# Moving most of the adaLN conditioning of a two-block transformer kernel into chunks beside later matrix products, with five smaller edits

## The chip, the cores and the metric

The kernel runs on 1 core of a Trainium2 chip. The metric is the device time of one execution in microseconds (us). A core has TensorE (PE: matrix products into the accumulator memory PSUM), VectorE (DVE), ScalarE (ACT), GpSimd (POOL), each with an instruction queue that is worked through in order, and the queue of SyncE (SP), which here only issues DMA transfers. The engines wait for each other with semaphores. TensorE's clock has two levels, 1.2 and 2.4 GHz; the profile gives the granted clock as a share of the upper one.

## The reference

Two transformer blocks follow each other on x (1 x 512 x 1024). The change touches the first block and a part of the second. The first, cut to what matters:

```python
def first_block(x, c, w_ada, b_ada, ...):
    mod = (silu(c) @ w_ada + b_ada)                    # 1024 -> 6 * 1024
    shift_m, scale_m, gate_m, shift_f, scale_f, gate_f = split(mod, 6)
    h = rmsnorm(x, norm_mix_w) * (1.0 + scale_m) + shift_m
    x = x + gate_m * hybrid_mixer(h, ...)
    h = rmsnorm(x, norm_mlp_w) * (1.0 + scale_f) + shift_f
    return rmsnorm(x + gate_f * (square(relu(h @ w_up)) @ w_down), norm_final_w)

def hybrid_mixer(h, ...):
    z, xbc, dt_raw, u_pool, gate_logits = split(h @ w_in, ...)   # 2048, 3072, 32, 1024, 2048 columns
    xbc = silu(causal_depthwise_conv(xbc, conv_w, conv_b))       # 4 taps
    dt = softplus(dt_raw + dt_bias)
    y = chunked_scan(xbc, dt, a_log) ; y = rmsnorm_by_group((y + d_skip * xs) * silu(z))
    y_ssd = y @ w_branch_ssd                                     # 2048 -> 1024
    pooled = means over windows of 2, 4, 8, 16 rows, minus u     # causal, 256 columns each
    y_pool = ((pooled @ pool_w by group) * pool_scale) @ w_branch_pool
    g_ssd, g_pool = split(sigmoid(gate_logits), 2)
    return (g_ssd * y_ssd + g_pool * y_pool) @ w_out
```

Only shift_m and scale_m are needed at the start; the other four parts of `mod` are first used behind the mixer. The second block is a sparse attention with a convolutional feed-forward, then a differential attention with 8 heads (its keys, values and queries are the product called qkv here) and another feed-forward.

## The kernel before

Activations lie with their features on the 128 partitions and the rows along the free axis. A matrix product is a `Linear` in the table `L`; it is made in groups of 128 output columns, in the order dt, xbc (24 groups), z (16), u (8), gates (16), bs (8), pw (8), bp (8), out, up0, down0, up1, down1, and then the second block. fp32 accuracy comes from three products of split operands: high times high, low times high, high times low. So a group over 1024 inputs is 8 x 3 = 24 matmuls of 512 rows. Each 128-column weight block is a unit: SP loads it into `w_raw` (two buffers), ACT copies its high part into `w_hi` (L428), DVE subtracts to get `w_lo` (L434). All three run two units ahead of TensorE. Counting semaphores keep them in step: `w_split` (a unit is split, its raw buffer free), `units_done` (TensorE has finished a unit), `evacuated` (a PSUM accumulator is free again). `evac_loop` is ACT's side of a product, `post_loop` DVE's, `products` TensorE's; POOL does elementwise work beside them.

The conditioning is `times_c`: the 6144 columns of `w_ada` come in 12 blocks of 512 columns, issued by POOL (L982). For each, DVE forms the sum over 8 row blocks of w times silu(c) in 8 linked steps, one `tensor_scalar` (L615) and seven `scalar_tensor_tensor` (L617); each linked step waits for the one before. TensorE's `modulation` (L1709) then adds over the partitions with four one-column matmuls against ones. Four blocks are made at the start, since h needs them; the other eight are spread over the 24 xbc groups, a third of a block per group. After xbc TensorE does their matmuls and waits for `mod_ready`, then for the last convolution (`conv_out`), and goes on to z. There DVE, POOL and ACT do the scan step by step beside the groups of z; a step needs the decay rows, which SP loads once the last convolution is written.

In gates, ACT's evacuation is a sigmoid (L1280), and POOL does the causal pooling (L1028 to L1036) from the start of the stage. In pw each group has only two row blocks (6 matmuls), but all 8 blocks of its weight buffer are split. ACT scales the accumulator into `et` (L1298), copies the high part (L1301), and DVE subtracts (L2390). qkv's groups all use accumulator banks 0 and 1 (L2033), so each waits for the evacuation of the one before (L1526, L1527). In the differential attention `turn_head` (L2151) transposes a finished head ahead of the next logits, and ACT's `head_out` copies it.

Of the kernel before, what the change touches and what calls it, by code (L numbers as in the profile page):

```python
# [15 lines left out]
P = 128  # L16
# [136 lines left out]
def two_block_program(nc, I, out):  # L153
    ctx = ExitStack()
    with ctx:
# [36 lines left out]
        def pcol(name, i=0):  # L192
# [17 lines left out]
                for i, a in enumerate((A_Z, A_Z + 16384, A_S + 8320, F + 24576))]  # L210
        ADA_FIRST = (2, 3, 0, 1)
        ada_acc = [at(f"ada_acc{i}", [P, 512], F32, A_MISC + (3 + i) * TILE if i < 4 else
                      A_S + 8320 + (i - 4) * 2048 if i < 9 else
                      A_MISC + (6, 3, 4)[i - 9] * TILE) for i in range(12)]
# [297 lines left out]
        def products(pe, l, ready, first=2, between=None, mid=None):  # L512
# [4 lines left out]
            for g in range(first):  # L517
# [91 lines left out]
        def times_c(dve, link, n, k0=0, k1=KD):  # L609

            u, slot, fill = (ADA_FIRST[n], n, 1) if n < 4 else (n, n % 2, n // 2)
            w, acc = wada[slot], ada_acc[u]
            if k0 == 0:
                dve.wait_ge(sem(f"ada_in{slot}"), 16 * fill)
                link(dve.tensor_scalar(acc[:], w[:, 0, :], small[:, 8:9], None, ALU.mult))  # L615
            for k in range(max(k0, 1), k1):
                ins = dve.scalar_tensor_tensor(acc[:], w[:, k, :], small[:, 8 + k:9 + k], acc[:], ALU.mult, ALU.add)  # L617
                if k < KD - 1:
                    link(ins)
                else:  # L620
                    ins.then_inc(sem("ada_acc"), 1)


# [236 lines left out]
        def _(sp):  # L860
# [65 lines left out]

            for name, l in L.items():
                if name == "z":
# [10 lines left out]
                    continue  # L939
                if name in ("ia", "oa1"):  # L940
# [27 lines left out]
        def _(pool):  # L968
# [7 lines left out]

            for n in range(12):
                u, slot = (ADA_FIRST[n], n) if n < 4 else (n, n % 2)
                if n >= 4:

                    pool.wait_ge(sem("ada_acc"), max(4, n - 1))
                pool.dma_start(wada[slot][:], I["w_ada"][0].rearrange("(k p) n -> p k n", p=P)[:, :, u * 512:u * 512 + 512]  # L982
                               ).then_inc(sem(f"ada_in{slot}"), 16)
# [143 lines left out]
        def _(act):  # L1127
            for t in range(NT):
                act.dma_start(xin[:, t, :], I["x"][0, t * P:(t + 1) * P, :]).then_inc(sem(f"x_in{t}"), 16)
            act.dma_start(metain[:], I["meta_tokens_2"]).then_inc(sem("meta_in"), 16)  # L1130
            act.sem_inc(sem("evacuated"), 2)
# [65 lines left out]
            def dt_steps(g):  # L1197
# [4 lines left out]
                elif g == 4:  # L1202
# [3 lines left out]
                elif g == 6:  # L1206
# [6 lines left out]
                elif g == 7:  # L1213
# [3 lines left out]
                      first=8, between=dt_steps, stop=8)  # L1217
            evac_loop(act, L["xbc"], conv_in, conv_silu, start=8)
# [74 lines left out]
            for g in range(KD):  # L1293
                l = L["pw"]
                act.wait_ge(sem("units_done"), l.U0 + g + 1)
                if g >= 2:
                    act.wait_ge(sem("pw_ready"), g - 1)
# [9 lines left out]
            act.wait_ge(sem("pw_ready"), KD)  # L1307
            evac_loop(act, L["bp"], branch_evac("bp"), mixed_hi)
            act.activation(HH[:, :, META - 2:META], modc[:, 24:32].unsqueeze(2).to_broadcast([P, KD, 2]), ACT.Copy)
# [204 lines left out]
            def project_out(g):  # L1514
# [3 lines left out]
                src = PS[:, 0:2, 0:TH]  # L1518
# [90 lines left out]
            for j in range(4):  # L1609
# [24 lines left out]
                for b in range(4):  # L1634
                    if j == 2 and b:
                        head_out(b - 1)
# [1237 lines left out]
```

## Time and profile before

| | |
|---|---|
| median of 3 runs | 2546.71 us (2544.07 to 2549.95) |
| the profiled execution | 2534.87 us, its span 2533.0 us |
| mean granted clock of TensorE | 0.974 |
| busy: PE, PEld, DVE, ACT, POOL | 94%, 84%, 55%, 42%, 16% |
| from HBM | 234.53 MB, 95 GB/s over the span |

The span is the time from the first to the last recorded instruction. PE is TensorE's matmuls, PEld its weight loads, which overlap them. A busy share is an average over stages with different limits; what an edit is worth is read from the stage that it touches.

### The profile page before, as it was taken

The page shows a single profiled execution, that of the slowest core. Times are in us where ns is not written, and L with a number is a line of the kernel's source. Part 1 is how long each engine was busy: PE and PEld are TensorE (multiplying, and loading weights), DVE is VectorE, ACT ScalarE, POOL GpSimd, SP SyncE. Part 2 cuts the span into 40 slices and gives each one's busy share as a digit, 9 for nine tenths or more (in the row PEclk, how much of TensorE's full clock was granted, in tenths as well). Part 3 has the DMA queues.
Part 4 walks back from the last instruction along what each step waited for, and adds up shares of the span by engine and source line. Part 5 has one row for each costly group of instructions (what it writes and reads, how often), then busy time and mean ns, then how long its engine had stood idle before and what let it go on. Part 6 is the DMA issues. An engine that isn't in the chain of part 4 may idle for free.

```text
span 2533.0 us, 41300 instructions
## 1 busy us (share of the span) xinstructions
PE 2392.3 (94%) x15423; PEld 2136.3 (84%) x15423; DVE 1386.4 (55%) x2101; ACT 1062.3 (42%) x1908; POOL 394.1 (16%) x350
## 2 busy tenths in 40 slices
PE   5899988999899999998989999999999989999998
PEld 4678867887689889886868999999878779999987
DVE  5886675423455335457854666643343445766621
ACT  5545863433544234323544433322455545333322
POOL 0000433711320010000121211100100001211100
PEclk8898998999999999999999999999999989999999
DMA  8464332332333353342201323333422112323332
GB/s 279 137 213 116 101 83 59 91 100 75 100 93 91 97 130 98 92 119 52 64 21 48 99 85 89 91 89 89 125 60 62 50 47 80 87 87 91 89 93 92
DMA packets 409384, 238.35 MB, mean 94 GB/s; under 512 B 11338, under 2 KB 400301, under 8 KB 409285
## 3 DMA queue, kind: packets, MB, share of 16 engines
q1 hardware_dynamic: 400453, 202.24, 28.7%
q0 software_dynamic: 8224, 32.61, 3.8%
q10 hardware_dynamic: 608, 2.16, 0.2%
q8 instruction: 64, 1.05, 0.2%
q14 instruction: 35, 0.29, 0.0%
HBM read 234.53 MB, written 5.00 MB: 95 GB/s over the span
## 4 chain that ended last, share of the span: by engine, by line
PE 81%; DVE 7%; ACT 4%; DMA 3%; issue 3%; POOL 0%; SPq 0%; DVEq 0%; POOLq 0%; ACTq 0%
PE PS L507 60%; PE PS L2033 5%; PE PS L1820 3%; DMA w_raw<-in_w_in_dram 1%; DVE ada_acc L617 1%; PE PS L1775 1%; PE PS L2164 1%; PE PS L2069 1%; PE PS L1835 1%; PE PS L2111 1%; ACT w_hi L428 1%; PE PS L1899 1%; DVE w_lo L434 1%; DVE conv_acc L2275 1%; DMA w_ada<-in_w_ada_dram 1%
## 5 line engine op out<-in xcount | busy, mean ns | idle before, releaser
L434 DVE TENSOR_TENSOR w_lo<-w_raw,w_hi 128x1024 fp32r<-128x1024 f32 (+1 forms) x376 | 474.4, 1262 | 637.7 <-ACT w_hi L428 636.5
L507 PE MATMUL PS<-op_hi,w_hi 128*128 128x264 f32 (+4 forms) x2456 | 608.2, 311 | 22.4 <-DVE w_lo L434 11.4
L507 PE MATMUL PS<-op_lo,w_hi 128*128 128x264 f32 (+4 forms) x2456 | 605.3, 310 | 0.0
L507 PE MATMUL PS<-op_hi,w_lo 128*128 128x264 f32 (+4 forms) x2456 | 603.0, 309 | 0.0
L428 ACT ACTIVATE w_hi<-w_raw 128x1024 fp32r<-128x1024 f32 (+1 forms) x376 | 382.8, 1018 | 313.5 <-PE PS L507 261.4
L507 PEld LDWEIGHTS PS<-op_hi,w_hi 128*128 128x128 f32 (+1 forms) x2456 | 399.6, 189 | 56.2 <-DVE w_lo L434 11.3
L507 PEld LDWEIGHTS PS<-op_hi,w_lo 128*128 128x128 f32 (+1 forms) x2456 | 398.9, 189 | 24.6 <-issue 0.8
L507 PEld LDWEIGHTS PS<-op_lo,w_hi 128*128 128x128 f32 (+1 forms) x2456 | 398.7, 189 | 23.4 <-issue 1.4
L507 PE MATMUL PS<-ff_hi,w_lo 128*128 128x512 f32 (+1 forms) x784 | 240.3, 343 | 0.0
L507 PE MATMUL PS<-ff_hi,w_hi 128*128 128x512 f32 (+1 forms) x784 | 239.9, 342 | 0.0
L507 PE MATMUL PS<-ff_lo,w_hi 128*128 128x512 f32 (+1 forms) x784 | 239.9, 342 | 0.0
L1488 ACT ACTIVATE ff_u<-PS 128x528 f32<-128x528 f32 x88 | 53.9, 613 | 334.4 <-PE PS L507 314.2
L603 POOL TENSOR_TENSOR ff_u<-ff_u,rstd 128x528 f32<-128x528 f32 x88 | 100.4, 1142 | 417.3 <-ACT ff_u L1488 389.9
L507 PEld LDWEIGHTS PS<-ff_lo,w_hi 128*128 128x128 f32 x784 | 135.6, 188 | 17.7
L507 PEld LDWEIGHTS PS<-ff_hi,w_lo 128*128 128x128 f32 x784 | 135.4, 188 | 17.7
L507 PEld LDWEIGHTS PS<-ff_hi,w_hi 128*128 128x128 f32 x784 | 135.6, 188 | 17.2
L673 POOL TENSOR_TENSOR sumsq<-sumsq,evac 128x528 f32<-128x528 f32 (+1 forms) x28 | 39.2, 1399 | 535.8 <-ACT evac L646 535.8
L2646 DVE SCALAR_TENSOR_TENSOR ff_c<-ff_u,param_cols,ff_c 128x528 f32<-128x528 f32 x88 | 70.4, 800 | 12.6 <-DVE ff_c L2645 6.7
L2645 DVE SCALAR_TENSOR_TENSOR ff_c<-ff_u,param_cols,ff_c 128x528 f32<-128x528 f32 x88 | 67.7, 769 | 12.7 <-DVE ff_c L2643 6.7
L2643 DVE TENSOR_SCALAR ff_c<-ff_u,param_cols 128x528 f32<-128x528 f32 x88 | 51.1, 580 | 25.7 <-DVE ff_c L2654 14.6
L617 DVE SCALAR_TENSOR_TENSOR ada_acc<-w_ada,small,ada_acc 128x512 f32<-128x512 f32 x84 | 63.1, 751 | 2.5
L701 POOL TENSOR_TENSOR resid<-resid,evac 128x512 f32 x16 | 20.7, 1292 | 278.5 <-ACT evac L635 278.5
(486 smaller groups left out, 3828.6 us busy)
## 6 DMA issues: line engine op xcount, KB each, us to landing
w_raw<-in_w_up_dram SPq DMA_DIRECT2D x120, 512.0 KB, 3.9
w_raw<-in_w_in_dram SPq DMA_DIRECT2D x64, 512.0 KB, 4.1
w_raw<-in_w_down_dram SPq DMA_DIRECT2D x64, 512.0 KB, 4.0
w_ada<-in_w_ada_dram POOLq DMA_DIRECT2D x12, 2048.0 KB, 10.3
decay<-sums_scratch SPq DMA_DIRECT2D x16, 512.0 KB, 5.1
w_raw<-in_w_branch_ssd_dram SPq DMA_DIRECT2D x16, 512.0 KB, 4.0
w_raw<-in_w_in_a_dram SPq DMA_DIRECT2D x16, 512.0 KB, 3.8
w_raw<-in_w_kv_b_dram SPq DMA_DIRECT2D x16, 512.0 KB, 3.9
```

The source lines that it names most:

```text
L428: act.activation(whi[slot][:, 0:ks, :], wraw[slot][:, 0:ks, :], ACT.Copy).then_inc(sem("w_hi_ready"), 1)
L434: dve.tensor_tensor(wlo[slot][:, 0:ks, :], wraw[slot][:, 0:ks, :], whi[slot][:, 0:ks, :].bitcast(F32), ALU.subtract).then_inc(sem("w_split ...
L507: last = pe.matmul(a[0:l.cols, h, 0:cn], w[slot][:, k, 0:l.cols], x[:, kk, c0:c0 + cn], start=(j == 0 and k == 0 and w is whi and x is l.h ...
L603: pool.tensor_tensor(x, x, rs[0:L[name].cols, :], ALU.mult).then_inc(sem("scaled"), 1)
L617: ins = dve.scalar_tensor_tensor(acc[:], w[:, k, :], small[:, 8 + k:9 + k], acc[:], ALU.mult, ALU.add)
L673: pool.tensor_tensor(sacc[:, c0:T], sacc[:, c0:T], et[g % 2][:, c0:T], ALU.add).then_inc(sem("sumsq_ready"), 1)
L1488: act.activation(halves(uu[par][:, 2:2 + T]), acc_view(l, par), ACT.Copy).then_inc(sem("evacuated"), 1)
L1820: last = pe.matmul(PS[0:rows, b + h, 0:TH], w[slot][:, k, 0:rows], x[:, k, h * TH:(h + 1) * TH], start=(k == 0 and w is whi and x is HH), ...
L2033: last = pe.matmul(PS[:, h, 0:TH], w[slot][:, k, :], x[:, k, h * TH:(h + 1) * TH], start=(k == 0 and w is whi and x is hi), stop=(k == KD ...
L2643: link(dve.tensor_scalar(c[:, :], u[:, 2:2 + T], w(2), pcol("conv_b_2", t + (x * 2 * NF + par * NF)), ALU.mult, ALU.add))
L2645: link(dve.scalar_tensor_tensor(c[:, :], u[:, 1:1 + T], w(1), c[:, :], ALU.mult, ALU.add))
L2646: dve.scalar_tensor_tensor(c[:, :], u[:, 0:T], w(0), c[:, :], ALU.mult, ALU.add).then_inc(sem("ff_conv"), 1)
```

## The change

- `w_ada`'s first four blocks are issued by ACT behind x and the meta tokens instead of by POOL beside them. Of the fourth, DVE sums row blocks 0 to 4 and TensorE adds blocks 5 to 7 by matmuls of the raw weights with the column silu(c).
- The other 4096 columns come as 32 chunks of 128 columns (`w_ada_cols`, two buffers), issued by SP between the weight loads of gates and bs and ahead of those of pw. DVE sums chunks 0 to 15 behind each `w_lo` of gates, and two per group of bs. TensorE adds chunk g-1 over the partitions behind group g of gates, two behind each group of bs but the first, which has one, and the last two behind group 1 of pw. `mod_ready` is awaited by ACT behind bp.
- dt and the first group of xbc are made together, row block by row block; the steps of dt on TensorE and ACT come two groups later.
- pw's high operand is copied straight from PSUM with its scale, the low operand computed from PSUM; the weights of pw are split over the two row blocks that are used.
- qkv's groups 0 to 3 alternate between two pairs of banks.
- `turn_head` and `head_out` come after the projection (or `partB`) of their step instead of before the logits.

The core of the diff:

```diff
-        def times_c(dve, link, n, k0=0, k1=KD):
...
+        BY_DVE = 5
+        def weighted_sum(dve, link, acc, w, rows):
+            link(dve.tensor_scalar(acc, w[:, 0, :], small[:, 8:9], None, ALU.mult))
+            for k in range(1, rows):
+                ins = dve.scalar_tensor_tensor(acc, w[:, k, :], small[:, 8 + k:9 + k], acc, ALU.mult, ALU.add)
+                if k < rows - 1:
+                    link(ins)
+            ins.then_inc(sem("ada_acc"), 1)
@@ SP
+            def ada_cols(n):
+                if n < 2:
+                    sp.wait_ge(sem("y_v"), NZ)
+                else:
+                    sp.wait_ge(sem("ada_acc"), 4 + n - 1)
+                c0 = 2 * D + n * P
+                sp.dma_start(wch[n % 2][:], I["w_ada"][0].rearrange("(k p) n -> p k n", p=P)[:, :, c0:c0 + P]).then_inc(
+                    sem(f"ada_in{n % 2}"), 16)
+                if name in ("gates", "bs"):
+                    for v in range(16):
...
+                        n = v - 2 + (16 if name == "bs" else 0)
+                        if n >= 0:
+                            ada_cols(n)
+                    continue
+                if name == "pw":
+                    for n in (30, 31):
+                        ada_cols(n)
@@ ACT
+            for n in range(4):
+                u = ADA_FIRST[n]
+                act.dma_start(wada[n][:], ...u * 512:u * 512 + 512]).then_inc(sem(f"ada_in{n}"), 16)
...
-                act.activation(et[g % 2][:, 0:S], acc_view(l, g % 2), ACT.Copy,
-                               scale=pcol("pool_scale", g)).then_inc(sem("evacuated"), 1)
-                act.wait_ge(sem("evacuated"), l.G0 + g + 3)
-                act.activation(PHh[:, g, :], et[g % 2][:, 0:S], ACT.Copy).then_inc(sem("pw_hi"), 1)
-                split_hi(act, l, g // 2, g % 2, 0)
+                act.activation(PHh[:, g, :], acc_view(l, g % 2), ACT.Copy, scale=pcol("pool_scale", g)).then_inc(
+                    sem("pw_hi"), 1)
+                split_hi(act, l, g // 2, g % 2, 0, 2 if g < 6 else 8)
@@ TensorE
+                if n == 3:
+                    pe.wait_ge(sem("ada_in3"), 16)
+                    for m in range(4):
+                        for k in range(BY_DVE, KD):
+                            pe.matmul(PS[:, m, 0:1], wada[n][:, k, m * P:(m + 1) * P], small[:, 8 + k:9 + k], ...)
+            def ada_cols(n):
+                pe.wait_ge(sem("ada_acc"), 4 + n + 1)
+                pe.matmul(bank(7)[:, n:n + 1], ch_acc[n % 2][:], ones[:, 0:1], start=True, stop=True).then_inc(
+                    sem("ada_done"), 1)
...
-            for n in range(4, 12):
-                modulation(n)
-            pe.wait_ge(sem("mod_ready"), 2)
...
+            products(pe, L["gates"], None, 16, lambda g: g and ada_cols(g - 1))
+            def bs_cols(g):
+                for n in ((15,) if g == 0 else (14 + 2 * g, 15 + 2 * g)):
+                    ada_cols(n)
+            products(pe, L["bs"], "y_ready", KD, bs_cols)
+            def last_cols(g):
+                if g == 1:
+                    ada_cols(30)
+                    ada_cols(31)
+            products(pe, L["pw"], "pooled_ready", between=last_cols)
...
-                pe.wait_ge(sem("evacuated"), l.G0 + g + 2)
+                b = 2 * (g % 2) if g < 4 else 0
+                pe.wait_ge(sem("evacuated"), l.G0 + g + (1 if 1 <= g <= 4 else 2))
@@ DVE
+            def ada_cols(n):
+                dve.wait_ge(sem(f"ada_in{n % 2}"), 16 * (n // 2 + 2))
+                if n >= 2:
+                    dve.wait_ge(sem("ada_done"), 4 + n - 1)
+                weighted_sum(dve, link, ch_acc[n % 2][:], wch[n % 2], KD)
+            post_loop(dve, L["gates"], after=lambda g, t, par: ada_cols(g), first=16)
...
-                dve.tensor_tensor(PHl[:, g, :], et[g % 2][:, 0:S], PHh[:, g, :].bitcast(F32), ALU.subtract).then_inc(
-                    sem("pw_ready"), 1)
+                dve.scalar_tensor_tensor(PHl[:, g, :], acc_view(L["pw"], g % 2), pcol("pool_scale", g),
+                                         PHh[:, g, :].bitcast(F32), ALU.mult, ALU.subtract).then_inc(
+                                             sem("evacuated"), 1)
```

## Rows read from the trace of the kernel before

**Rows 1.** the chain of work that ended last, shares of the span
```profile
PE 81%; DVE 7%; ACT 4%; DMA 3%; issue 3%; POOL 0%; SPq 0%; DVEq 0%; POOLq 0%; ACTq 0%
```

**Rows 2.** timeline of the start: start us, us, engine, line [idle, releaser]
```profile
17.23 0.49 DVE L615 TENSOR_SCALAR ada_acc<-w_ada,small 128x512 f32<-128x512 f32 x1 [17.23 <-DMA w_ada<-in_w_ada_dram]
...
35.54 5.47 DVE L617 SCALAR_TENSOR_TENSOR ada_acc<-w_ada,small,ada_acc 128x512 f32<-128x512 f32 x7
...
41.07 1.87 PE L1709 MATMUL PS<-mats,ada_acc 128*128 128x1 f32 x8 [3.96 <-DVE ada_acc L617]
```

**Rows 3.** busy time in stretches: us, engines, clock, DMA share, GB/s
```profile
25.00:30.00 5.00, 1.76 (x9) 1.79 (x10) 4.79 (x8) 5.00 (x8) 0.00 (x0) 0.50 1.05 402
...
35.00:40.00 5.00, 2.11 (x19) 2.03 (x19) 4.79 (x8) 1.83 (x4) 0.00 (x0) 0.93 0.01 4
...
40.00:45.00 5.00, 1.87 (x8) 1.78 (x8) 4.04 (x9) 0.90 (x2) 1.75 (x2) 0.50 0.37 99
```

**Rows 4.** the chain in order of time: start us, us, what
```profile
77.95 3.35 DVE dtT L2295
...
213.79 5.05 DMA decay<-sums_scratch
...
227.17 2.00 PE PS L1775 x16
...
241.14 5.56 PE PS L507 x24
```

**Rows 5.** groups of 53 to 213.7: line, engine, shapes xcount | busy, mean ns
```profile
L617 DVE SCALAR_TENSOR_TENSOR ada_acc<-w_ada,small,ada_acc 128x512 f32<-128x512 f32 x54 | 40.5, 750 | 1.4
...
L434 DVE TENSOR_TENSOR w_lo<-w_raw,w_hi 128x1024 fp32r<-128x1024 f32 x25 | 30.6, 1224 | 23.7 <-ACT w_hi L428 23.4
```

**Rows 6.** who waited for whom, 53 to 128: us in total, times, longest
```profile
PE PS L1726 <- DVE dtT L2303: 10.1, 1, 10.1
```

**Rows 7.** busy time of each engine from 457 to 515
```profile
457.00:515.00 58.00, 58.00 (x253) 47.00 (x251) 16.14 (x11) 23.44 (x27) 53.02 (x46) 1.00 0.39 98
```

**Rows 8.** VectorE's groups over the whole span, one of 144 columns
```profile
L2732 DVE SCALAR_TENSOR_TENSOR probsB<-probsB,statsB,probsB 128x144 f32<-128x144 f32 x8 | 2.8, 350 | 0.0
```

**Rows 9.** timeline of ACT and DVE in the first gates groups
```profile
463.41 0.60 ACT L1280 ACTIVATE z<-PS 128x512 f32 x1 [2.76 <-PE PS L507]
...
464.99 1.26 DVE L434 TENSOR_TENSOR w_lo<-w_raw,w_hi 128x1024 fp32r<-128x1024 f32 x1 [3.08 <-ACT w_hi L428]
...
468.94 1.28 ACT L1280 ACT_TABLE_LOAD   x1 [3.98 <-PE PS L507]
...
471.81 2.13 DVE L434 TENSOR_TENSOR w_lo<-w_raw,w_hi 128x1024 fp32r<-128x1024 f32 x1 [5.55 <-ACT w_hi L428]
```

**Rows 10.** line L2369 (ns min/median/max), and its timeline
```profile
L2369 DVE SCALAR_TENSOR_TENSOR z<-z,param_cols,rstd x8: 739/1482/1793, 326.3 to 423.0; 128x512 f32<-128x512 f32 x8
...
418.49 6.27 DVE L2369 SCALAR_TENSOR_TENSOR z<-z,param_cols,rstd 128x512 f32<-128x512 f32 x4
...
446.30 2.74 DVE L2369 SCALAR_TENSOR_TENSOR z<-z,param_cols,norm_v 128x512 f32<-128x512 f32 x4
```

**Rows 11.** timeline from the end of bs to the start of bp
```profile
628.27 0.60 ACT L1286 ACTIVATE evac<-PS 128x512 f32<-128x512 f32 x1 [4.46 <-PE PS L507]
...
651.11 0.47 PE L507 MATMUL PS<-pool_hi,w_hi 128*128 128x512 f32 x1 [1.98 <-ACT evac L1298]
```

**Rows 12.** DMA issues of 600 to 660, KB each, us to landing
```profile
w_raw<-in_w_branch_pool_dram SPq DMA_DIRECT2D x4, 512.0 KB, 3.8
...
w_raw<-in_pool_w_dram SPq DMA_DIRECT2D x8, 128.0 KB, 2.1
```

**Rows 13.** TensorE's timeline in qkv's first groups
```profile
1798.48 0.52 PE L2033 MATMUL PS<-op_hi,w_hi 128*128 128x264 f32 x2 [2.15 <-ACT evac L1527]
...
1814.01 0.52 PE L2033 MATMUL PS<-q_op_hi,w_hi 128*128 128x264 f32 x2 [1.20 <-ACT norm_v L1527]
```

**Rows 14.** who waited for whom, 1938 to 2113
```profile
PE PS L2151 <- ACT v_tokB L1573: 8.1, 2, 4.3
```

More of the change, by code:

```diff
@@ L510, in products_of, with products @@
                 last.then_inc(sem("units_done"), 1)
-        def products(pe, l, ready, first=2, between=None, mid=None):
+        def products(pe, l, ready, first=2, between=None, mid=None, start=0):
             if ready:
@@ L516, in products @@
             first = l.groups if l.kbase else min(first, l.groups)
-            for g in range(first):
+            for g in range(start, first):
                 products_of(pe, l, g // 2, g % 2, ready if g < 2 or l.kbase else None, None if g else mid)
@@ L1216, in _ @@
             evac_loop(act, L["xbc"], conv_in, lambda g, t, par: (g, t, par) != (0, 0, 0) and conv_silu(g, t, par),
-                      first=8, between=dt_steps, stop=8)
-            evac_loop(act, L["xbc"], conv_in, conv_silu, start=8)
+                      first=10, between=dt_steps, stop=10)
+            evac_loop(act, L["xbc"], conv_in, conv_silu, start=10)
             conv_silu(NX, NX // 2, 0)
@@ L1634, in _ @@
                 for b in range(4):
-                    if j == 2 and b:
-                        head_out(b - 1)
-                    if not more and b in (1, 2):
-                        head_hi(3 + b)
                     exps(j, b, 0)
@@ L1643, in _ @@
                         part_splitB(b)
+                    if j == 2 and b:
+                        head_out(b - 1)
+                    if not more and b in (1, 2):
+                        head_hi(3 + b)
                     if b >= 2:
@@ L1716, in _ @@
             pe.wait_ge(sem("x_turned"), 2 * KD)
-            products(pe, L["dt"], "h_ready")
+            for u in range(2):
+                pe.wait_ge(sem("w_split"), u + 3)
+            for k in range(KD):
+                pe.wait_ge(sem("h_ready"), k + 1)
+                for u, l in enumerate((L["dt"], L["xbc"])):
+                    for w, x in ((whi, HH), (whi, HL), (wlo, HH)):
+                        last = pe.matmul(acc_view(l, 0, l.cols), w[u][:, k, 0:l.cols], x[:, k, META:T],
+                                         start=(k == 0 and w is whi and x is HH), stop=(k == KD - 1 and w is wlo))
+                    if k == KD - 1:
+                        last.then_inc(sem("units_done"), 1)
             def dt_steps(g):
                 a_tok = dtok[:, 1, :, :].rearrange("p t h -> p (t h)")
-                if g == 4:
+                if g == 6:
                     pe.wait_ge(sem("dt_done"), 1)
@@ L1736, in dt_steps @@
                     last.then_inc(sem("dt_sums"), 1)
-            products(pe, L["xbc"], None, 6, dt_steps)
-            for n in range(4, 12):
-                modulation(n)
-            pe.wait_ge(sem("mod_ready"), 2)
+            products(pe, L["xbc"], None, 8, dt_steps, start=1)
             pe.wait_ge(sem("dt_tok"), 4)
@@ L2194, in _ @@
                 for b in range(4):
-                    if j == 2 and b:
-                        turn_head(b - 1)
-                    if not more and b in (1, 2):
-                        turn_head(3 + b)
                     logitsB(j, b, 0)
@@ L2203, in _ @@
                         partB(b)
+                    if j == 2 and b:
+                        turn_head(b - 1)
+                    if not more and b in (1, 2):
+                        turn_head(3 + b)
                     logitsB(j, b, 1)
@@ L2314, in _ @@
                 dt_steps(g)
-                n, third = 4 + g // 3, g % 3
-                times_c(dve, link, n, *((0, 2), (2, 5), (5, 8))[third])
-            dve.wait_ge(sem("ada_done"), 12)
-            link(dve.tensor_tensor(modc[:, 16:48], bank(7)[:, 16:48], PC[:, 16:48], ALU.add))
-            r = ROWS["norm_mlp_w"]
-            dve.scalar_tensor_tensor(aff[:, 8:16], modc[:, 32:40], 1.0, PC[:, r:r + 8], ALU.add, ALU.mult).then_inc(
-                sem("mod_ready"), 1)
             def by_head(ap):
```

89 lines of the change are left out of this document (45 added, 44 removed).

## The prediction

> **What bounds the kernel now.** I read the page first. TensorE is busy for 94% of the span, and the chain of work that ended last runs over it for 81% [rows 1]. So an edit pays only where TensorE stands still, and it costs wherever it makes TensorE stand still anew. Then I read the stages that the diff touches, and in each the wait that ends last.
>
> *Start.* VectorE begins the first weighted sum at 17.23 us, when the first `w_ada` block has landed, ends the fourth at 41.0, and TensorE ends its last `modulation` matmul at 42.94 [rows 2]. The loads run at about 400 GB/s and are through before 35 us [rows 3]. So the start is bound by VectorE, behind a late first landing.
>
> *xbc, 45.6 to 213.7 us.* A group of 24 matmuls takes TensorE 5.56 us [rows 4]. VectorE does per group one `w_lo` (1.22), three conv steps of the length of a `times_c` step (0.75), and 2.7 `times_c` steps on average [rows 5]: about 5.8 with gaps, so here VectorE sets the pace. The softplus work (its reciprocal alone is 3.35 us [rows 4]) makes TensorE stand 10.1 us before its dt transposes [rows 6].
>
> *What follows xbc.* TensorE also waits for eight `modulation` calls, until 217.7. But the chain shows another path: conv end, decay rows landing 213.79 to 218.84, the decay exponentials, `mT`, and the first L1775 matmul at 227.17 [rows 4]. That is 13.4 us after the last conv, whatever the modulation does. The wait for `mod_ready` is hidden by it.
>
> *gates.* TensorE never stops. VectorE has one `w_lo` per group and lies idle otherwise. But POOL is busy for 53 of the 58 us from 457 to 515, with 46 operations (the causal pooling) [rows 7].
>
> **Part by part, against the profiled execution (span 2533.0, own time 2534.87).**
>
> 1. *x first, `w_ada` behind it in ACT's queue, fourth block split.* The first block lands when x, the constants and itself are in. In rank order I put that at 14.7 us: some 5 MB at 0.39 MB/us, and 2 us. This is an estimate from [rows 3]; if they mix as now, it is 17.2. The fourth block can't land before about 34 us, as the bytes are the same. VectorE then owes 5 rows (0.5 + 4 x 0.79 = 3.7 us), TensorE 12 matmuls for the other three rows and 4 to close. Four such matmuls take 1.87 us [rows 2] at a granted clock of 0.50, the lower level [rows 3], and I put half for the upper: 7.5 us for the 16 at the lower, 4 at the upper. End 39 to 42 instead of 42.94, then two more small additions (0.4). Gain 0.5 to 4.5, I take 2.5. POOL's queue loses its loads, so ACT issues four more, about 2 us, beneath the wait for x.
>
> The Trainium skill (DMA: Bandwidth & Descriptors, Queues, rings and completion order) says that an engine takes turns between queue rows and consumes one row in ring order. By that x would come ahead of `w_ada` and the estimate of 14.7 stands; no row here shows the two in one queue.
>
> 2. *xbc without `times_c`, dt and the first group interleaved, dt steps two groups later.* 600 matmuls at 5.56/24 us are 139. Added: the lower clock of the first nine (2), dt transposes and sums (2.5), stalls at groups 5 and 6, where VectorE's 4.7 and 4.6 us of softplus still overrun (0.8 + 2.5), and the tail of evacuation, `w_hi`, `w_lo`, three conv steps and silu (6.7). Sum 154 against 168.1: gain 14 (bounds 10, if dt still waits; 18, if no stall is left). All of it moves the decay chain forward. The removal of the eight modulations adds nothing, as said.
>
> 3. *32 chunks in gates, bs and pw.* (a) TensorE: one such matmul per chunk, 0.23 us by the same halving; formerly under cover, now on the path: 32 x 0.25 = 8. (b) VectorE's sum over 128 columns: the nearest row, 144 columns, is 0.350 us [rows 8]; so about 0.33 each and 0.035 for the link, 8 operations 2.9 us. TensorE waits after group g for chunk g-1. From units_done: table load and sigmoid, `w_hi`, `w_lo`: 2.87 us without the load, 4.1 with it (the load from 468.94, `w_lo` from 471.81, its free length 1.23 [rows 9]; it comes every second group). With 2.9 that is 5.8 and 7.0 against a group of 5.8: a stall of 1.2 us every second group. (c) POOL. While POOL works, `scalar_tensor_tensor` L2369 takes 1.48 us at the median instead of 0.75: four take 6.27 us at 418.49 and 2.74 at 446.30, when POOL is idle [rows 10]. So each is held 0.88 us, about the length of one POOL operation; `w_lo` shows it too (2.13) [rows 9]. The new sums are eight such operations with short bodies. I price a hold of 0.8 for each: 0.365 + 0.8 = 1.17; 8 x 1.17 + 1.85 for `w_lo` = 11.2 us of VectorE per group while POOL pools. POOL's stretch stays near 57 us, five groups. VectorE then sets the pace: chunk 4 ends 58.4 us after the first gate group, TensorE is through group 6 at 64.2 instead of 33.4. Loss 31. The ten others lose 0.25 + 0.6 each (8.5). gates: 38 with overlaps taken off. Bounds: 13.6 (no hold: 16 x 0.25 + 8 x 1.2) and 42 (full hold, and the clock falls in the stalls).
>
> The Trainium skill (GPSIMD Engine Reference, Specifications) says that GpSimd's SBUF interfaces are shared with VectorE, with contention for VectorE instructions with two SBUF inputs. The new `scalar_tensor_tensor` has two. The trace agrees (1.48 against 0.75 us); the page gives no length. By the rule taken as absent for short operations the stage would lose 13.6, by rule and row 38.
>
> (d) bs: VectorE owes per group of two units 2.5 + 0.7 + 5.8 and one hold of 0.9 = 9.9 us, in 10.9; the next `w_lo` comes 0.1 to 0.2 late. With two matmuls (0.5) a group: 5 (bounds 4 and 9).
>
> 4. *pw.* Now bs end (628.2) to bp start (651.1) is 22.9 us [rows 11]. Direct operands and 2-row splits alone would bring it to about 16.4: two groups per 3.2 us, paced by the 2.1 us landing of each small weight, then 3.8 for bp's first [rows 12], `w_hi` and `w_lo`. But SP now holds pw's first loads until chunk 29 is summed, so they land about 1.9 us after bs ends; and VectorE does chunks 30 and 31 (5.8 us) ahead of pw's first operand, while TensorE's `last_cols` waits for them. Step by step: pw 2 starts 13.5 us after bs ends, bp at 26.5. Loss 3.6 (bounds -3 and 6). Queued behind: POOL's gate work, which has slack.
>
> 5. *qkv on two accumulators.* The waits of 2.15 and 1.20 us for the evacuation go [rows 13]: gain 3.4. The one before the head squares stays.
>
> 6. *Heads turned after the projection.* Waits of 8.1 us in all before `turn_head`, one in each of the last two head pairs [rows 14], get 6 and 3 us of products ahead of them. But the softmax chain beside them then ends last. Gain 1 to 8, I take 5.
>
> Sum: -2.5 - 14 + 38 + 5 + 3.6 - 3.4 - 5 = +21.7 us, so 2556.6 for the profiled execution. The median of the runs, 2546.71, lies 0.5% above that execution; on it I add the same: 2568.
>
> **Rivals.**
>
> *Half the hold.* Short operations slip into the gaps between POOL's: 0.4 each, 8 us of VectorE per group. gates costs 26, the whole +10: 2557. For it: the pauses of POOL between operations. Against: both uncovered stretches of L2369 show the hold at every operation.
>
> *No hold.* gates costs 13.6, the whole about -3: 2543. For it: no short two-input operation of before met POOL in a row. Against: the held part of L2369 is the wait, not the body.
>
> *Faster.* The place is again TensorE's wait for the chunks. If a sum is so short that it fits the 1.7 us left under a group with a table load, only the matmuls stay: gates 4, bs 4, and the whole -17: 2530. The sign turns where gates costs less than 16, a hold of some 0.1 to 0.15 us per operation. It needs 128 columns well under the 0.35 us of the row.
>
> *The page's rule* is the forecast's mechanism, with no price of its own.
>
> **How the numbers follow.** Forecast 0.60 (own range 2556 to 2586), half the hold 0.16, no hold 0.16, faster 0.08. Above 2541 lies all but the last case and part of the third; the range is 2541 to 2586. Within 0.2% (5 us, what measuring can tell here) falls about half of "no hold": same 0.08, faster 0.14, slower 0.78.
>
> **What would show it.** Right: in the gates, until POOL's pooling ends, `scalar_tensor_tensor` of 128 columns at 1.1 to 1.2 us and TensorE idle before the chunk's matmul for 4 to 6 us a group; after it 0.33 us and stalls near 1 us every second group; the last conv some 16 us earlier; xbc paced by TensorE at 5.6 us; the wait for L1298's evacuation gone and one of 5 to 6 us for the chunks at pw; no wait between qkv 0 and 1. Wrong: short sums in the gates at 0.33 us all along, or a clock that stays low through the stalls, or `w_ada` landing much later from ACT's queue.

## The result and the profile after

| | before | after |
|---|---|---|
| median of the runs | 2545.39 us (2536.98 to 2549.95) | 2589.59 us (2587.88 to 2592.04) |
| ratio | | 1.0182, interval 1.0155 to 1.0209 |
| profiled execution, its span | 2534.87, 2533.0 us | 2587.88, 2585.2 us |
| mean granted clock of TensorE | 0.974 | 0.966 |

The change makes the kernel slower, as forecast, but by 44 us (52 by the two spans) instead of 22, outside the range. This account is read off TensorE's timeline: the first matmul of each stage in both traces, and the difference of the lengths. "To mT" ends where the first L1775 (now L1805) starts, the scan's first product with the matrix `mT`; "u" is the product that makes u_pool.

```
stage                        before     after  difference  forecast
start, to the first product    45.60     57.37     +11.8      -2.5
first product to mT           181.57    171.56     -10.0     -14
mT to u                       172.15    175.37      +3.2       0
u                              52.66     52.63       0.0       0
gates                          88.96    125.13     +36.2     +38
bs                             87.21     90.94      +3.7      +5
end of bs to bp                22.96     30.22      +7.3      +3.6
bp, out, first feed-forward   449.67    451.68      +2.0       0
attention A                   274.71    280.07      +5.4       0
second feed-forward           414.68    413.39      -1.3       0
qkv groups 0 to 3              34.88     30.99      -3.9      -3.4
the rest of attention B       288.52    285.11      -3.4      -5
tail                          419.38    420.72      +1.3       0
sum                                                +52.2     +21.7
```

*Start.* The timeline (start us, us, engine, line) answers to [rows 2]:

```profile
3.29 16.84 ACTq L1143 DMA_DIRECT2D w_ada<-in_w_ada_dram  x4
20.23 1.28 ACT L1147 ACT_TABLE_LOAD   x1 [20.23 <-issue]
...
27.70 0.18 DVE L2282 RECIPROCAL small<-small 128x4 f32<-128x4 f32 x1 [27.70 <-ACT small L1154]
27.79 0.46 DVE L613 TENSOR_SCALAR ada_acc<-w_ada,small 128x512 f32<-128x512 f32 x1
...
47.36 5.26 PE L1724 MATMUL PS<-small,w_ada 128*128 128x1 f32 x24
...
57.37 0.61 PE L1747 MATMUL PS<-op_hi,w_hi 128*32 128x512 f32 x1 [3.04 <-DVE op_lo L2308]
```

ScalarE's queue stands on its four new issues for 16.84 us. Its first operation came at 3.48 us before; now it comes at 20.23. One by one the four issues took 0.49, 2.71, 4.33 and 9.22 us. Silu, squares and root follow late, the reciprocal waits for them, and the first sum waits behind the reciprocal: 27.79 instead of 17.23.

*From xbc to u.* Who waited for whom in TensorE, 57 to 229 (in all, times, longest), and the chain, which answers to [rows 4]:

```profile
PE PS L1784 <- ACT xbc L1197: 6.7, 1, 6.7
PE PS L507 <- DVE w_lo L434: 5.6, 3, 2.4
PE PS L1805 <- DVE mT L2377: 5.6, 1, 5.6
```

```profile
119.51 83.63 PE PS L507 x360
215.31 5.29 DMA decay<-sums_scratch
...
228.93 3.68 PE PS L1805 x16
232.60 1.81 PE PS L1810 x2
```

The wait of 10.1 us for dt [rows 6] is gone and TensorE sets the pace of xbc (83.63 / 15 = 5.58 us a group). Behind it TensorE stands 6.7 and then 5.6 us, and the first sixteen L1805 matmuls take 3.68 us, where the same sixteen took 2.00 [rows 4]. The granted clock is 0.50 from 229 to 233; in the kernel before it is 1.00 from 227 to 231, where a product of z ran right up to them.

*Gates.* Line L615 from 460 to 517, with GpSimd's pooling, and from 520 to 582, without it (ns min/median/max); then the groups of 462 to 517 (busy us, mean ns), which answer to [rows 8]; then a pair of groups in the timeline:

```profile
L615 DVE SCALAR_TENSOR_TENSOR ada_cols<-w_ada_cols,small,ada_cols x39: 350/622/1464, 468.1 to 516.0; 128x128 f32<-128x128 f32 x39
...
L615 DVE SCALAR_TENSOR_TENSOR ada_cols<-w_ada_cols,small,ada_cols x63: 350/352/353, 526.1 to 581.4; 128x128 f32<-128x128 f32 x63
```

```profile
L615 DVE SCALAR_TENSOR_TENSOR ada_cols<-w_ada_cols,small,ada_cols 128x128 f32<-128x128 f32 x39 | 30.5, 782 | 1.4
L434 DVE TENSOR_TENSOR w_lo<-w_raw,w_hi 128x1024 fp32r<-128x1024 f32 x6 | 8.1, 1342 | 10.4 <-ACT w_hi L428 10.4
```

```profile
484.51 1.97 DVE L434 TENSOR_TENSOR w_lo<-w_raw,w_hi 128x1024 fp32r<-128x1024 f32 x1 [3.30 <-ACT w_hi L428]
486.41 1.06 DVE L613 TENSOR_SCALAR ada_cols<-w_ada_cols,small 128x128 f32<-128x128 f32 x1
487.50 5.45 DVE L615 SCALAR_TENSOR_TENSOR ada_cols<-w_ada_cols,small,ada_cols 128x128 f32<-128x128 f32 x7
...
493.00 0.59 PE L1734 MATMUL PS<-mats,ada_cols 128*128 128x1 f32 x2 [5.65 <-DVE ada_cols L615]
```

Free, a sum takes 352 ns; under the pooling 782 on the mean. A chunk there takes 6.5 us instead of 2.95. Its first operation, which reads one block and a column, is held as well (1.06 us in the lines shown, 0.28 without GpSimd). TensorE stands 5.65 us for it, and the 24 products behind the wait take 7.84 us instead of 5.6, at a granted clock of 0.69 from 493 to 501.3. Over 462 to 517 the clock is 0.83; it was 1.00 in that stretch [rows 7]. VectorE also stands, 3.30 us for `w_hi`, which waits for those products.

*End of bs to bp*, answering to [rows 11, 12]:

```profile
676.26 1.06 ACT L428 ACTIVATE w_hi<-w_raw 128x1024 fp32r<-128x1024 f32 x1 [11.42 <-DMA w_raw<-in_pool_w_dram]
...
678.67 0.77 PE L507 MATMUL PS<-op_hi,w_hi 128*128 128x512 f32 x1 [5.33 <-ACT evac L1300]
...
687.27 0.59 PE L1734 MATMUL PS<-mats,ada_cols 128*128 128x1 f32 x2 [2.53 <-DVE ada_cols L615]
...
688.31 0.76 PE L507 MATMUL PS<-op_hi,w_hi 128*128 128x512 f32 x1 [0.45 <-DVE pool_lo L2436]
```

bs ends at 673.0. The first small weight lands 3.1 us later, and pw's third group (the prediction's pw 2, counted from 0) waits for both chunks and starts at 688.31.

### The profile page after: what moved, and what is told of

Read it like the earlier page. It is cut to its first block, busy times and chain, and to the rows that moved or that the text cites. A ratio compares the mean times of both kernels' runs of the same rounds, so it can differ in the third digit from the quotient of the medians.

```text
span 2585.2 us, 41306 instructions
## 1 busy us (share of the span) xinstructions
PE 2418.0 (94%) x15447; PEld 2153.4 (83%) x15447; DVE 1434.7 (55%) x2292; ACT 1051.7 (41%) x1900; POOL 381.8 (15%) x338
## 4 chain that ended last, share of the span: by engine, by line
PE 80%; DVE 8%; ACT 4%; issue 4%; DMA 2%; ACTq 1%; POOL 0%; SPq 0%; POOLq 0%; DVEq 0%
PE PS L507 58%; PE PS L2073 5%; PE PS L1859 3%; DVE ada_cols L615 2%; PE PS L1805 1%; ACT w_hi L428 1%; DMA w_raw<-in_w_branch_ssd_dram 1%; PE PS L2109 1%; PE PS L2204 1%; PE PS L1874 1%; PE PS L2151 1%; PE PS L1938 1%; ACTq L1143 1%; DVE w_lo L434 1%; PE PS L1974 1%
## 5 line engine op out<-in xcount | busy, mean ns | idle before, releaser
L434 DVE TENSOR_TENSOR w_lo<-w_raw,w_hi 128x1024 fp32r<-128x1024 f32 (+2 forms) x376 | 464.4, 1235 | 612.6 <-ACT w_hi L428 611.7
L507 PE MATMUL PS<-op_hi,w_hi 128*128 128x264 f32 (+3 forms) x2440 | 604.7, 312 | 21.8 <-DVE w_lo L434 15.0
L507 PE MATMUL PS<-op_lo,w_hi 128*128 128x264 f32 (+3 forms) x2440 | 601.2, 310 | 0.0
L507 PE MATMUL PS<-op_hi,w_lo 128*128 128x264 f32 (+3 forms) x2440 | 599.8, 310 | 0.0
L428 ACT ACTIVATE w_hi<-w_raw 128x1024 fp32r<-128x1024 f32 (+2 forms) x376 | 378.9, 1008 | 318.2 <-PE PS L507 258.6
L507 PEld LDWEIGHTS PS<-op_hi,w_hi 128*128 128x128 f32 x2440 | 400.3, 190 | 50.0 <-issue 10.5
L507 PEld LDWEIGHTS PS<-op_hi,w_lo 128*128 128x128 f32 x2440 | 399.4, 190 | 23.6
L507 PEld LDWEIGHTS PS<-op_lo,w_hi 128*128 128x128 f32 x2440 | 398.1, 190 | 22.6 <-issue 0.7
L615 DVE SCALAR_TENSOR_TENSOR ada_cols<-w_ada_cols,small,ada_cols 128x128 f32<-128x128 f32 x224 | 95.6, 427 | 7.9
```

The lines of the kernel that those rows point to most:

```text
L428: act.activation(whi[slot][:, 0:ks, :], wraw[slot][:, 0:ks, :], ACT.Copy).then_inc(sem("w_hi_ready"), 1)
L434: dve.tensor_tensor(wlo[slot][:, 0:ks, :], wraw[slot][:, 0:ks, :], whi[slot][:, 0:ks, :].bitcast(F32), ALU.subtract).then_inc(sem("w_split ...
L507: last = pe.matmul(a[0:l.cols, h, 0:cn], w[slot][:, k, 0:l.cols], x[:, kk, c0:c0 + cn], start=(j == 0 and k == 0 and w is whi and x is l.h ...
L615: ins = dve.scalar_tensor_tensor(acc, w[:, k, :], small[:, 8 + k:9 + k], acc, ALU.mult, ALU.add)
```

## Experiments

Spans are compared with 2585.2 (after) or 2533.0 us (before), ratios go against the kernel before on the same chip. Each kernel is the changed one with the edit shown, unless it says otherwise. Executions of one kernel differ: the spans of the kernel before lie between 2530.4 and 2548.7 us on four chips, and the intervals of runs 1, 2 and 6 overlap that of the change. So what these say rests on the lengths of single stages, which repeat much better where TensorE does not wait (gates without chunks: 88.96 or 88.97 us in six traces).

**1. w_ada issued by GpSimd**

```diff
@@ ACT
-            for n in range(4):
-                act.dma_start(wada[n][:], ...)
@@ POOL, where the kernel before has it
+            for n in range(4):
+                pool.dma_start(wada[n][:], ...)
```

(The chunks' loads then count on another semaphore.)

> The changed kernel with one thing undone: the first four w_ada blocks are issued by GpSimd again, as in the kernel before; the fourth block stays split between VectorE and TensorE and the reciprocal stays ahead of the sums. In the changed kernel ScalarE's queue stands on these four issues from 3.29 to 20.2 us, and its first operation comes at 20.23 instead of 3.48. Theory A (the issue holds ScalarE): ScalarE is free at 3.5 us again, the sums begin near 17 us, the first product comes at 43 to 46 us instead of 57.4, and the whole is 11 to 14 us under the changed kernel. Theory B (what costs is that the blocks land behind x, whoever issues them): the first sum begins after 25 us and less than 4 us come back. Theory C (the reciprocal ahead of the sums costs): the first sum still waits for it, 17 to 23 us, and about half comes back.

Span 2572.9 (-12.3), ratio 1.0149 [1.0121, 1.0176].

```profile
16.71 0.18 DVE L2282 RECIPROCAL small<-small 128x4 f32<-128x4 f32 x1 [16.71 <-ACT small L1154]
17.01 0.49 DVE L613 TENSOR_SCALAR ada_acc<-w_ada,small 128x512 f32<-128x512 f32 x1
...
36.63 5.26 PE L1724 MATMUL PS<-small,w_ada 128*128 128x1 f32 x24
41.75 1.84 PE L1729 MATMUL PS<-mats,ada_acc 128*128 128x1 f32 x8
...
46.64 0.60 PE L1747 MATMUL PS<-op_hi,w_hi 128*32 128x512 f32 x1 [3.04 <-DVE op_lo L2308]
```

Theory A holds: the issues were the cost, neither the order of landing nor the reciprocal. The rest of the edit gains nothing here: VectorE is through by 38.4 instead of 41.0, but TensorE's share of the fourth block starts at 36.63 and ends at 43.59, and the first product comes at 46.64, 1.0 later than before.

**2. w_ada issued by SyncE**

```diff
@@ SP, behind c and the constant matrices
+            for n in range(4):
+                sp.dma_start(wada[n][:], ...)
```

> The changed kernel with the first four w_ada blocks issued by the load queue of SyncE, behind c and the constant matrices, instead of by ScalarE. Theory A (the four issues hold any such queue for some 17 us, and it matters that ScalarE has the squares behind them and SyncE only parameters and the first weights, wanted from 30 us on): SyncE stands 15 to 18 us in them, ScalarE begins at 3.5 us, the sums at 14 to 18 us, the first product comes at 46 to 50 us, 8 to 12 us come back. Theory B (the hold belongs to ScalarE's queue alone, behind its own x loads): SyncE issues them in about 2 us, and the start is as with GpSimd, 11 to 13 us come back. Theory C (parameters and weights come too late): under 4 us come back.

Span 2578.6 (-6.6), ratio 1.0169 [1.0152, 1.0185]; first product at 52.15.

```profile
1.89 15.81 SPq L861 DMA_DIRECT2D w_ada<-in_w_ada_dram  x4
...
16.06 0.49 DVE L613 TENSOR_SCALAR ada_acc<-w_ada,small 128x512 f32<-128x512 f32 x1 [1.34 <-DMA w_ada<-in_w_ada_dram]
...
17.74 5.20 SPq L871 DMA_DIRECT2D param_rows<-in_b_ada_dram  x1
...
36.04 1.28 PE L1714 MATMUL PS<-mats,param_rows 128*128 128x128 f32 x5 [8.47 <-DMA param_rows<-in_kn_b_dram]
```

The hold belongs to the issues and not to ScalarE: SyncE stands 15.81 us, and 5.20 more on the next small one. Nothing that VectorE needs stands behind them here, but the parameters do, and TensorE waits 8.47 us for those. So about half comes back (5.2 us at the first product, 57.37 against 52.15), between theories A and C.

**3. No chunks**: all calls of `ada_cols` and their loads left out.

> The changed kernel with the 32 chunks left out altogether (their loads, sums and matmuls; the feed-forward conditioning is then the bias alone, so that part of the computation is left out). Theory A (the chunks carry the loss, with the start): gates takes no stall, bs 87 us, pw about 16 us from the end of bs to bp, so 30 + 5 + 14 = 49 us come back, half of the last by the direct operands; against the kernel before the rest is +12 at the start, -10 in xbc, -6 in pw, -5 in qkv, -4 in the heads, thus some 5 to 13 us faster than before. Theory B (the changed kernel is slower all over, through the clock or the moved code): the stages behind bp stay 2 to 7 us behind, and under 40 us come back.

Span 2532.8 (-52.4), ratio 0.9979 [0.9961, 0.9996]. gates takes 88.96 us, as before; bs to its end 87.21; end of bs to bp 18.8. So the chunks cost 36.2 + 3.7 + 11.4 = 51 us, and the direct operands alone gain 4.2 in pw, which the chunks had hidden. Theory A in its main part: 52 us come back of 49 expected, but against the kernel before the span is 0.2 us shorter and the ratio 0.2% lower, where 5 to 13 us were expected.

**4. No pooling on GpSimd**

```diff
-                    link(pool.tensor_tensor(dst[:, PAD:UPW], src[:, PAD:UPW], ...
...
+                pool.sem_inc(sem("pooled"), 1)
```

> The changed kernel in which GpSimd leaves out the causal pooling (its 46 operations; the pool operand is then the unpooled projection, so that part of the computation is left out), and the chunks stay. Theory A (GpSimd's operations hold VectorE's sums): a pair of gate groups takes 13.2 us from the first on instead of 19 to 20, a chunk takes 2.95 us instead of 6.7, and 19 to 21 us come back. Theory B (the first six groups are slow through their loads, the table loads or the low clock): the chunks stay above 5 us there and under 5 us come back.

Span 2572.7 (-12.5), ratio 1.0128 [1.0100, 1.0156]. gates takes 107.35 us, 17.8 less than after; 3.2 of the difference in attention A go the other way.

```profile
482.12 0.28 DVE L613 TENSOR_SCALAR ada_cols<-w_ada_cols,small 128x128 f32<-128x128 f32 x1
482.44 2.68 DVE L615 SCALAR_TENSOR_TENSOR ada_cols<-w_ada_cols,small,ada_cols 128x128 f32<-128x128 f32 x7
```

The hold is GpSimd's. In gates it costs 17.8 us (19 to 21 were expected); 18.4 us stay without any of it.

**5. TensorE three chunks behind**

```diff
-        ch_acc = [... for i in range(2)]
+        ch_acc = [... for i in range(4)]
-            products(pe, L["gates"], None, 16, lambda g: g and ada_cols(g - 1))
+            products(pe, L["gates"], None, 16, lambda g: g > 2 and ada_cols(g - 3))
```

(bs and pw follow with two chunks more in arrears.)

> The changed kernel in which TensorE adds a chunk three groups after it was issued instead of one (four sum buffers in place of two). Theory A (of the gates' loss, 8 us are TensorE's wait for the sum of the group before, 1.4 us every second group behind a table load; the rest under the pooling is VectorE's own length): the stall is gone in the last ten groups, pairs of 11.6 instead of 13.25 us; under the pooling the pairs go from 19 or 20 to 17.5 or 18.5 us; 10 to 14 us come back. Theory B (VectorE's work sets the pace in all sixteen groups): under 4 us come back. Theory C (TensorE's wait is all that costs, as six slow chunks would fit into the time of sixteen groups): over 20 us.

Span 2564.6 (-20.6), ratio 1.0121 [1.0094, 1.0149]. gates: 104.16 us, 21.0 less than after. The groups of 462 to 517, and two groups in the timeline:

```profile
L615 DVE SCALAR_TENSOR_TENSOR ada_cols<-w_ada_cols,small,ada_cols 128x128 f32<-128x128 f32 x45 | 36.3, 806 | 1.6
```

```profile
489.30 1.21 DVE L434 TENSOR_TENSOR w_lo<-w_raw,w_hi 128x1024 fp32r<-128x1024 f32 x1
490.44 0.27 DVE L613 TENSOR_SCALAR ada_cols<-w_ada_cols,small 128x128 f32<-128x128 f32 x1
490.75 6.25 DVE L615 SCALAR_TENSOR_TENSOR ada_cols<-w_ada_cols,small,ada_cols 128x128 f32<-128x128 f32 x7
496.93 1.21 DVE L434 TENSOR_TENSOR w_lo<-w_raw,w_hi 128x1024 fp32r<-128x1024 f32 x1
```

The sums are held as before (806 ns), yet 21 us come back, more than theory A's 10 to 14. That is theory C's figure, but not its mechanism: 15.2 us stay against the 88.96 of before, so TensorE's wait is not all that costs. VectorE now works almost without a pause, 7.63 us in the group shown, and that sets the pace under the pooling; in the changed kernel it idled too. The last six groups take 5.8 us each, as theory A had it. What the lag took away is the loop: TensorE waits for the chunk, `w_hi` for TensorE, `w_lo` for `w_hi`, the next chunk for `w_lo`.

**6. pw's loads and operands ahead of the last two chunks**

```diff
@@ SP: pw's first two weights, then chunks 30 and 31
@@ DVE
+            ada_cols(30)
+            ada_cols(31)
             dve.wait_ge(sem("ada_done"), 36)
@@ TensorE: the two are added behind bp's group 0
```

> The changed kernel with the last two chunks moved behind pw: SyncE loads pw's first two weights ahead of chunks 30 and 31, VectorE sums the two after pw's operands, and TensorE adds them after bp's first group. Theory A (from the end of bs to bp 30.2 us instead of 18.8 without chunks, because the loads land late and two sums of 5.9 us in all lie ahead of pw's second group): the stretch falls to 19 to 22 us, 8 to 11 us come back. Theory B (the small loads and the splits pace pw anyway): under 3 us. Theory C (the two sums now hold bp's weights): the stretch falls but bp stalls by 2 to 5 us.

Span 2573.7 (-11.5), ratio 1.0155 [1.0136, 1.0174]. End of bs to bp: 18.72 us instead of 30.22, as without any chunks. Theory A, slightly beyond its figure, and in bp TensorE waits only 0.62 us, at the second of the two chunks.

**7. Three mended together**: runs 1, 5 and 6 in one kernel.

> The changed kernel with three things undone or mended together: w_ada issued by GpSimd, TensorE adding a chunk three groups later (four buffers), and the last two chunks behind pw. Theory A (the three losses are apart and add): 12.3 + 20.6 + 9 = 42 us under the changed kernel, so a span near 2543 and 10 us over the kernel before; what stays is the hold under GpSimd's pooling and 32 matmuls. Theory B (the lag has already taken in the pw part, or the losses overlap): 30 to 36 us come back. Theory C (better than the kernel before): a span under 2530.

Span 2549.6 (-35.6), ratio 1.0037 [1.0021, 1.0053]. Up to bp it is 40.5 us earlier than after (662.68 against 703.22), close to theory A's sum; attention A then takes 283.3 us instead of 280.1, and the whole span comes out inside theory B's 30 to 36. So even mended, the chunks lose against the kernel before.

**8. Three edits on the kernel before**: direct pooled operands, two qkv accumulators, heads turned after the projection.

> The kernel before with only three of the edits: the pooled operands straight from PSUM with two-row splits, the first qkv groups on two accumulators, the heads turned after the projection. The conditioning, the start and xbc stay as before. Theory A (these three pay by themselves, and what they give is not taken back): from the end of bs to bp 18.8 us instead of 23.0 as in the run without chunks, 3.9 us in qkv, 2 to 3.5 in the head pairs, in all 10 us (0.4%) under the kernel before. Theory B (part is given back in attention A, where the clock lies lower in every variant so far, by 3 to 10 us): 0 to 6 us. Theory C (the pw edit pays only where xbc and the gates are changed too): bs to bp stays near 23.

Span 2524.8 (-8.1), median 2528.81, ratio 0.9956 [0.9938, 0.9973]. End of bs to bp 18.4 (-4.6), qkv 31.0 (-3.9), the rest of attention B 283.9 (-4.6), attention A 277.9 (+3.2). Faster than both kernels; theory A with a part of B.

**9. Half in xbc, half as chunks**, on the kernel of run 8

```diff
-                n, third = 4 + g // 3, g % 3
-                times_c(dve, link, n, *((0, 2), (2, 5), (5, 8))[third])
+                n, sixth = 4 + g // 6, g % 6
+                times_c(dve, link, n, *((0, 2), (2, 3), (3, 4), (4, 6), (6, 7), (7, 8))[sixth])
...
+            post_loop(dve, L["gates"], after=lambda g, t, par: g >= 12 and ada_cols(g - 12), first=16)
+                for n in range(2 if g < 6 else 0):
+                    ada_cols(4 + 2 * g + n)
```

> The kernel before with the three edits of the run with three edits, and half of the feed-forward conditioning moved: channels 2048 to 4095 stay in xbc as four 512-column blocks (spread over 24 groups, dt steps two groups later), channels 4096 to 6143 become 16 chunks, four in the last four gate groups, where GpSimd's pooling is over, and two in each of the first six groups of bs; TensorE adds them two or three groups later; none lies ahead of pw. Theory A (VectorE sets the pace of xbc only because it owes eight blocks there; a chunk costs little where GpSimd is still and TensorE does not wait for the newest): xbc gains 8 to 11 us, gates lose 1, bs 4: 4 to 7 us under the run with three edits (span 2524.8), so about 2519. Theory B (what xbc gains is taken back, by the clock behind the longer wait for mT and by the chunks): within 2 us of it. Theory C (slower than it).

Median 2528.66, ratio 0.9951 [0.9934, 0.9967]: the same as run 8. gates starts 3.6 us earlier (447.50 against 451.08, not the 8 to 11 of theory A: TensorE still waits 8.7 us for the dt transposes), bs gives 3.3 back (90.5 against 87.2), attention A takes 280.2. Theory B by the figure; its clock part is not isolated.

**10, 11. The kernel before, merely later**

```diff
             for n in range(1, 4):
                 times_c(dve, link, n)
+            for _ in range(8):      # 20 in the second
+                link(dve.memset(sqt[:, 0:512], 0.0))
```

> The kernel before with eight dummy fills of 512 columns on VectorE behind its fourth block sum; nothing else is changed. It asks whether the stretches that no edit touches (attention A took 274.7 us before and 277.6 to 284.5 in the variants) take another time merely because they begin at another moment. Theory A (the difference comes from the edits' own work, such as other buffers): the first product comes 2 to 4 us later, and each later stretch has its length of before within 1 us. Theory B (the granted clock behind short waits depends on when they come): the start moves by 2 to 4 us and attention A takes 3 us or more longer, with its waits unchanged.

> The same as the run before it with twenty dummy fills, so a start 5 to 9 us later. Theory A: each later stretch has its length of before within 1 us. Theory B: attention A takes yet another length, 275 to 285 us.

The first product comes 4.5 and 12.8 us later, the end 15.0 and 16.9 us later (one profile each, spans 2548.0 and 2549.8). Attention A takes 282.4 and 278.7 us instead of 274.7, gates 88.96 us in both, as before. Theory A fails: an untouched stretch has another length. But theory B's cause, the later start, is not shown. Nine executions of the kernel before on the same chip have spans of 2535.5 to 2544.5 us; with 4.5 or 12.8 us added they reach 2540 to 2549 and 2548 to 2557, and the two spans measured lie inside. So ordinary differences between executions explain them as well.

**12. Heads alone, on the kernel before**

> The kernel before with only the heads turned after the projection (ScalarE's matching order with it). All stages ahead of the last two head pairs are those of before and begin at the same moments, so the stretch from the third qkv group pair on is compared undisturbed. Theory A (the waits before turn_head, 8.1 us in all, are mostly filled): from the tenth stretch of projections on 3 to 6 us less, and 0 to 6 us for the whole, at the edge of what can be told. Theory B (the softmax chain beside them ends last): under 1.5 us less in the trace.

Ratio 0.9990 [0.9973, 1.0007]. From 1890.69 (now 1900.07) to the end of the head pairs: 221.7 us instead of 222.9. The wait of [rows 14] is gone, and these have come:

```profile
PE PS L2069 <- DVE statsB L2713: 1.6, 1, 1.6
...
PE PS L2113 <- ACT o_tok L1579: 1.2, 1, 1.2
PE PS L2113 <- DVE q_op_lo L2766: 1.1, 1, 1.1
```

Theory B: 1.1 us. This kernel also runs the same instructions as the kernel before up to attention B, and begins attention A 1.0 us later. Attention A took 282.7 us all the same, so 8 us of difference need hardly any shift. TensorE over the whole stretch (busy, x, then the other engines, granted clock, DMA), first in the kernel before, then in this one:

```profile
1100.00:1376.00 276.00, 246.12 (x1706) 212.59 (x1707) 175.74 (x432) 116.97 (x287) 35.04 (x41) 0.96 0.21 56
```

```profile
1101.00:1385.00 284.00, 257.99 (x1706) 221.99 (x1707) 175.98 (x432) 117.62 (x287) 35.03 (x41) 0.92 0.21 54
```

The same 1706 matmuls keep TensorE busy 12 us longer at a clock of 0.92 instead of 0.96. What sets the clock apart in two traces of the same instructions stays open.

## Why the prediction was wrong, step by step

Of the 30.5 us between forecast and trace the start has 14.3, xbc with what follows it 7.2, pw 3.7, the untouched stages 7.4, the heads 1.6; gates, bs and qkv came out 3.6 us better.

*The start: the step that failed.* "ACT issues four more, about 2 us, beneath the wait for x" should have read 16.84 us with all of ScalarE behind it. The 2 us were carried over from x's own four issues of 512 KB each; the w_ada blocks have 2 MB each. Runs 1 and 2 show it. Size alone is not the reason: the first 2 MB issue took 0.49 us and the fourth 9.22, and in the kernel before one 512 KB issue of SyncE, at 12.91 us behind GpSimd's 8 MB, took 10.67. That row would have warned me. It fits a hold that grows with what is already queued; no run isolates it, and from GpSimd no issue took more than 1.05 us. That x lands first was right: TensorE's transposes begin at 11.31 us instead of 14.07. The Trainium skill (DMA: Bandwidth & Descriptors, Queues, rings and completion order) says that a queue row is consumed in ring order; the trace agrees by these two times. I also named the danger at the end ("w_ada landing much later from ACT's queue") in the wrong form: what was late was not the block but ScalarE.

*xbc.* Forecast gain 14, measured 10.0, TensorE waits three times for `w_lo`, 5.6 us in all, where I had two stalls of 3.3 us, and the group behind the last wait takes 7.37 us at the lower clock. "The removal of the eight modulations adds nothing" was wrong with the other sign: TensorE now stands 6.7 and 5.6 us ahead of the scan steps, and mT to u takes 3.2 us more, of which the first L1805 and L1810 show 2.6. This is not one trace's accident: mT to u takes 174.8 to 177.2 us in the eight traces without modulations behind xbc, 171.7 to 172.8 in the five with all eight, 173.5 in run 9 with four. I argue, but no run isolates, that the removed matmuls had kept the clock up.

*gates.* 38 forecast, 36.2 measured: luck, by two errors that cancel. The hold is 0.43 us an operation (782 against 352 ns), not 0.8, so VectorE owes 7.6 us a group (run 5) instead of 11.2. That is the price of my rival "half the hold". But that rival gave 26 us, because I let each engine run at its own length; the loop between TensorE, `w_hi`, `w_lo` and the chunk adds idle time on both sides, and over the pooling the granted clock is 0.83 instead of 1.00 (0.97 in runs 4 and 5). Run 5 keeps the hold and opens the loop: 15.2 us. Run 4 takes the hold away and keeps the loop: 18.4. The ten groups without pooling lost 10.6 us (13.25 instead of 11.12 a pair), forecast 8.5. The Trainium skill (GPSIMD Engine Reference, Specifications) states contention with GpSimd for VectorE instructions with two SBUF inputs; run 4 agrees, where seven such sums take 2.68 us without GpSimd's operations, against 5.45. In the rival called faster my own terms add up to -13.3 and not -17, unless pw's loss of 3.6 goes too, which I did not say.

*bs* 3.7 for 5: right. *pw* 7.3 for 3.6: the steps were right (late loads, two chunks ahead of the third group) and each came out larger: landing 3.1 us after the end of bs instead of 1.9, third group after 15.3 instead of 13.5, bp after 30.2 instead of 26.5. Run 6 shows that all of it, 11.5 us, was the order.

*qkv* 3.9 for 3.4: right. *Heads*: forecast 5; 1.1 us by run 12 where nothing else differs. 3.4 to 4.6 in the other kernels are not separated from the scatter below.

*What no step held.* 7.4 us lie in stages that no edit touches, 5.4 in attention A. Runs 10 to 12 show that these stages take another time in another execution with the same instructions: over the fourteen traces attention A took 274.7 (before, the shortest) to 284.5 us. Whether the moment at which they begin decides it is not shown. So the profiled execution of before, 10.5 us under its kernel's median where that of after lies 1.7 under, was a lucky one to compare with, and that is why the medians differ by 44 us and the spans by 52.

## What to carry to other kernels

Before an issue is moved to another engine's queue, read what that queue holds behind it, and don't carry a price over from another size or another queue: the same four issues took 3.70 us from GpSimd, 15.81 from SyncE and 16.84 from ScalarE. Look for the longest single issue of that kind of queue while the DMA engines are full, and count it as work. Where one engine's result is wanted by the other in the same round, price the loop and not the two lengths, and let the consumer lag by two or three buffers. Spare time under a product is only spare if no third engine holds the operations put there and no small load or operand of the next stage queues behind them.

## What the hardware showed unexpectedly

Four issues of 2 MB each, in pieces of 2 KB, held ScalarE's sequencer for 16.84 us (0.49, 2.71, 4.33, 9.22) and SyncE's for 15.81 (0.43, 2.04, 7.92, 5.29); from GpSimd the four took 3.70 us in the kernel before. VectorE's 128-column sums with two SBUF inputs took 352 ns free and 782 to 806 ns on the mean beside GpSimd, up to 1464. An unchanged stretch of short waits (attention A) took 274.7 to 284.5 us from trace to trace; in the two traces shown, at granted clocks of 0.96 and 0.92. As spans of the kernel before went from 2530.4 to 2548.7 us, a single trace can't tell a difference under some 10 us unless the stages are compared one by one.
